# A two-block transformer step on one core: the experts' conditional branch passed before the last product, the tail split by column halves, and low parts, sines and row numbers in other places

## The reference

```python
def first_block(x, ...):
    for i in range(2):
        h = gated_deltanet(x, ...) if i == 0 else swa_sink_attention(x, ...)
        x = layer_norm(ALPHA * x + h, ln_g[i, 0], ln_b[i, 0])
        f = swiglu(x, ...) if i == 0 else moe_swiglu(x, ...)
        x = layer_norm(ALPHA * x + f, ln_g[i, 1], ln_b[i, 1])
    return x

def moe_swiglu(x, w_router, w_gate, w_up, w_down):
    top_val, top_idx = lax.top_k(xf @ w_router, 2)
    gates = ...                       # softmax of the two, one row per token
    for e in range(8):
        h = silu(xf @ w_gate[e]) * (xf @ w_up[e])
        out = out + gates[:, e:e + 1] * (h @ w_down[e])

def second_block(x, positions, ...):
    cos_a, sin_a = rope_tables(positions, 128)
    cos_i, sin_i = rope_tables(positions, 64)
    for l in range(2):
        h = rmsnorm(x, norm_g[l])
        q, k, v, ga, iq, ik, iw, xr, gr, ma, mb = split(h @ w_in[l])
        ...
        x = x + merged @ w_o[l]
    return rmsnorm(x, final_g)
```

## Time and profile before

| | us |
|---|---|
| median of 3 runs (lowest, highest) | 2206.4 (2204.94, 2208.66) |
| the profiled execution | 2202.83 |
| its span, first to last instruction | 2201.0 |
| PE busy | 2128.4 |
| VectorE busy | 1742.1 |
| ScalarE busy | 1483.7 |
| GpSimd busy | 378.1 |
| stage of the experts (560 to 1460): PE busy in 900 | 894.64 |
| 1460 to 1490: PE busy in 30 | 19.20 |

### The profile page before, as it was taken

How to read it: one execution, slowest core, us unless ns; L and a number is a source line. 1 busy time by engine, 2 the same in 40 slices (tenths; PEclk the granted TensorE clock), 3 DMA queues, 4 the chain that set the end, 5 groups by cost and what they waited for, 6 DMA issues and landing times.

```text
span 2201.0 us, 34517 instructions
## 1 busy us (share of the span) xinstructions
PE 2128.4 (97%) x13871; PEld 1888.9 (86%) x13871; DVE 1742.1 (79%) x2200; ACT 1483.7 (67%) x1982; POOL 378.1 (17%) x338
## 2 busy tenths in 40 slices
PE   8999999889999999999999999989998999999998
PEld 7988999877877888888888888869898998899898
DVE  5756555888999999999999999975698665689675
ACT  5644444556787888888888888864687844477864
POOL 0511000001002000000000000000667500458710
PEclk9999999998999999999999999989999999999999
DMA  8225855429999999999999999966555475555552
GB/s 278 97 76 122 264 192 179 157 71 349 356 336 387 395 388 390 370 394 378 376 366 394 372 390 375 386 218 202 177 172 177 129 228 184 184 159 175 158 165 98
DMA packets 326878, 564.69 MB, mean 257 GB/s; under 512 B 19872, under 2 KB 160952, under 8 KB 326712
## 3 DMA queue, kind: packets, MB, share of 16 engines
q1 hardware_dynamic: 314560, 527.60, 67.9%
q0 software_dynamic: 11760, 34.76, 5.7%
q10 hardware_dynamic: 392, 0.05, 0.0%
HBM read 548.32 MB, written 14.02 MB: 255 GB/s over the span
## 4 chain that ended last, share of the span: by engine, by line
PE 78%; DVE 10%; issue 6%; ACT 4%; POOL 1%; DMA 1%; SPq 0%; DVEq 0%; ACTq 0%; POOLq 0%
PE bank L901 24%; PE bank L903 23%; PE bank L902 23%; DVE parts L2626 3%; PE bank L907 2%; PE bank L1056 1%; ACT parts L1947 1%; PE bank L1874 1%; DVE work L3429 1%; POOL scr_f L811 1%; DVE work L3432 0%; PE bank L1834 0%; ACT work L2557 0%; DVE work L3430 0%; PE bank L1855 0%
## 5 line engine op out<-in xcount | busy, mean ns | idle before, releaser
L2626 DVE TENSOR_TENSOR parts<-raw,parts 128x1024 fp32r<-128x1024 f32 (+2 forms) x711 | 856.2, 1222 | 320.6 <-ACT parts L1947 297.3
L1947 ACT CAST parts<-raw 128x1024 fp32r<-128x1024 f32 (+2 forms) x711 | 730.5, 1036 | 404.2 <-PE bank L903 389.2
L901 PE MATMUL bank<-cols,parts 128*128 128x256 f32 x1680 | 488.9, 291 | 11.3 <-DVE work L3542 4.9
L902 PE MATMUL bank<-cols,parts 128*128 128x256 f32 x1680 | 477.8, 284 | 0.0
L903 PE MATMUL bank<-cols,parts 128*128 128x256 f32 x1680 | 477.6, 284 | 0.0
L2626 DVE TENSOR_TENSOR fast<-raw,fast 128x1024 fp32r<-128x1024 f32 x302 | 361.8, 1218 | 29.7 <-ACT fast L1947 12.9
L1947 ACT CAST fast<-raw 128x1024 fp32r<-128x1024 f32 x302 | 315.5, 1052 | 85.7 <-PE bank L903 77.3
L901 PEld LDWEIGHTS bank<-cols,parts 128*128 128x128 f32 x1680 | 323.5, 193 | 18.6 <-issue 9.9
L902 PEld LDWEIGHTS bank<-cols,parts 128*128 128x128 f32 x1680 | 323.9, 193 | 2.8 <-issue 1.9
L903 PEld LDWEIGHTS bank<-cols,parts 128*128 128x128 f32 x1680 | 323.7, 193 | 0.0
L901 PE MATMUL bank<-parts,cols 128*128 128x512 f32 x740 | 292.2, 395 | 8.0 <-DVE cols L3088 3.5
(11 more groups left out here) (433 smaller groups left out, 3385.4 us busy)
## 6 DMA issues: line engine op xcount, KB each, us to landing
raw<-in_moe_w_gate_dram SPq DMA_DIRECT2D x112, 1024.0 KB, 8.5
raw<-in_moe_w_up_dram SPq DMA_DIRECT2D x112, 1024.0 KB, 8.4
raw<-in_moe_w_down_dram SPq DMA_DIRECT2D x112, 1024.0 KB, 8.9
raw<-in_w_in_dram SPq DMA_DIRECT2D x76, 1024.0 KB, 5.3
raw<-in_a_w_in_dram SPq DMA_DIRECT2D x12, 1024.0 KB, 11.5
raw<-in_ffn_w_gate_dram SPq DMA_DIRECT2D x11, 1024.0 KB, 5.3
raw<-in_ffn_w_up_dram SPq DMA_DIRECT2D x11, 1024.0 KB, 5.4
raw<-in_ffn_w_down_dram SPq DMA_DIRECT2D x11, 1024.0 KB, 5.0
```

The source lines that it names most:

```text
L901: pe.matmul(o, l[0], r[0], start=start, stop=False)
L902: pe.matmul(o, l[0], r[1], start=False, stop=False)
L1947: a.copy(dst[0], src).then_inc(*up(o + "hi", x))
L2626: v.tensor_tensor(dst[1], src, dst[0].bitcast(F32), ALU.subtract).then_inc(*up(o + "lo", x))
```

## The change

1. **Branch.** In `experts` the last step's down product (`down(NS - 1)`) and, on VectorE, `scatter_last` are no longer in the loop but in a function `last`, which is called in the `If` arm and in a new `Else` arm, on ScalarE and VectorE. The sum of (1, 1) is a function of its own. `Signals.rewind` sets the counters back so that both arms count alike. PE's queue keeps its `If` where it was.
2. **Row numbers.** `ids` stands ahead of the last four pieces' low parts and of `product`, and waits for ScalarE's pt in place of PE's p_picked.
3. **Sines.** More `yield`s: ScalarE's sines come one step behind VectorE's angles, the second angles one step later than before.
4. **The norm behind the experts.** Both means first; the second half's LayerNorm product between the first half's gain and diagonal; the second half's gain on GpSimd (event h_rows_p); low parts and column parts alternate; PE calls `h_cols(0, 1)` inside `rm_first`, behind the third piece.
5. **First mixer.** The low parts of the pieces behind `T_qv[3]` and `T_qv[4]` (`POOL_LO`, two pieces) are GpSimd's, ahead of `level(0)`; who reads them waits for pool_lo.
6. **Tail.** The last `out_proj` does the last four pieces of t=1 by column halves (event quarter behind the first); sum, gain and squares of t=1 follow by halves (`f_deviation`).

```diff
@@ Signals
+    def rewind(self, before):
+        for family, n in before.items():
+            if not family.startswith("o_") and "_o_" not in family:
+                self.count[family] = n
@@ pieces
+    POOL_LO = W.after[T_qv[3]] + W.after[T_qv[4]]
+    def lo_name(x):
+        return "pool_lo" if x in POOL_LO else "lo"
@@ sync_program, load
-                sp.wait_ge(*at(o + "lo", W_.chunks[c - RAW]["pieces"][-1]))
+                for x in W_.chunks[c - RAW]["pieces"][-2:]:
+                    sp.wait_ge(*at(lo_name(x) if o == MAIN else o + "lo", x))
@@ pool_program
         gp.memset(N1.TT[HIGH, :, 0:64], 0.0).then_inc(*up("tt_zero"))
+        gp.wait_ge(*at("tt_zero"))
+        for y in POOL_LO:
+            src, dst = piece_view(W, y)
+            gp.wait_ge(*at("hi", y))
+            gp.tensor_tensor(dst[1], src, dst[0].bitcast(F32), ALU.subtract).then_inc(*up("pool_lo", y))
         gp.wait_ge(*at("gdn_const"))
-        gp.wait_ge(*at("tt_zero"))
         level(0)
...
+        gp.wait_ge(*at("h_gain", 0))
+        gp.wait_ge(*at("rows", 3, 1))
+        gp.tensor_tensor(HN.G[0][:, 1, :], X[:, 1, :], HN.g[0], ALU.mult).then_inc(*up("h_rows_p", 0, 1))
@@ tensor_program, out_proj
             k_.then_inc(*up("half", mine[7]))
+            if by_half:
+                for h, event in ((0, "quarter"), (1, "used")):
+                    for k in range(4, 8):
+                        k_ = step(k, 1, (h,))
+                    k_.then_inc(*up(event, mine[7]))
+                return
@@ tensor_program, second block
             if l == 0:
                 h_cols(0, 0)
-                h_cols(0, 1)
...
-            rm_first(..., ("v", l, 0), (lambda: h_cols(1, 1)) if l else None)
+            rm_first(..., ("v", l, 0), lambda l=l: h_cols(l, 1))
@@ scalar_program, experts
-            for n in range(NS + 3):
+            for n in range(NS + 1):
...
-                if 2 <= n <= NS + 1:
+                if n > 1:
                     down(n - 2)
-            return flag
+            return flag, lambda: down(NS - 1)
@@ scalar_program, setup_steps
+            yield
             yield
             for i in range(2):
                 ...
                 a.activation(co, rr, ACT.Sin).then_inc(*up("cos", i))
                 yield
+                yield
...
+        before = dict(S.count)
         with a.If(flag > 0):
+            last()
             ...
+        S.rewind(before)
+        with a.Else():
+            last()
         root_table(3)
@@ scalar_program, h_norm
+            h_deviation(l, 0)
             if l == 0:
+                his(1, 4)
+                h_hi(0, 0)
+                h_deviation(0, 1)
+                h_hi(0, 1)
+                his(4, 5)
@@ scalar_program, the end
+        def f_deviation():
+            q = LT[:, 8:16]
+            a.wait_ge(*at("resid", 1, 1, 0))
+            a.activation(HN.junk[:, 0:512], X[:, 1, 0:512], ACT.Square, accum_out=q[:, 0:1]).then_inc(*up("h_ss", 2, 1, 0))
+            a.wait_ge(*at("h_ss", 2, 1, 0))
+            a.activation(q[:, 1:2], q[:, 0:1], ACT.Identity, bias=eps["h"], scale=1.0 / D).then_inc(*up("h_ss", 2, 1, 1))
+            a.wait_ge(*at("resid", 1, 1, 1))
+            a.activation(HN.junk[:, 512:1024], X[:, 1, 512:1024], ACT.Square, accum_out=q[:, 6:7]).then_inc(*up("h_ss", 2, 1))
+            a.wait_ge(*at("h_ss", 2, 1))
+            a.activation(q[:, 7:8], q[:, 6:7], ACT.Sqrt, bias=q[:, 1:2], scale=1.0 / D).then_inc(*up("h_sd", 2, 1))
@@ vector_program, experts
             def ids(e):
-                v.wait_ge(*at("p_picked", e))
+                v.wait_ge(*at("pt", e))
...
+                if side and n == 0:
+                    ids(0)
+                if side and ahead and g == 3:
+                    ids(e + 1)
                 if n < NS:
                     for x in gu[n][4:8]:
                         after(x, W_, o)
                     product(n)
-                if side and n == 0:
-                    ids(0)
-                if side and ahead and g == 3:
-                    ids(e + 1)
...
+            def last():
+                down(NS - 1)
+                scatter_last(NE - 1)
+            return flag, last
@@ vector_program, behind the experts
+        S.rewind(before)
+        with v.Else():
+            last()
+            add_last(MAIN, NE - 1, 1, 1)
...
+        ln_mean(0)
+        ln_mean(1)
         ln_gains(0)
-        ln_gains(1)
         ln_rows(0)
         h_gains(0, 0)
+        ln_gains(1)
         h_diag(0, 0)
+        h_lows(0, 0, 1)
         ln_rows(1)
-        h_gains(0, 1)
...
@@ vector_program, the end
+                if l == t == 1:
+                    for h, event in enumerate(("quarter", "used")):
+                        cs = slice(512 * h, 512 * h + 512)
+                        v.wait_ge(*at(event, t_["o"][7]))
+                        v.tensor_tensor(X[:, t, cs], X[:, t, cs], bank[6 + h][:, :], ALU.add).then_inc(*up("resid", l, t, h))
+                        v.wait_ge(*at("resid", l, t, h))
+                        v.tensor_tensor(HN.G[2][:, t, cs], X[:, t, cs], HN.g[2][:, cs], ALU.mult).then_inc(*up("h_rows", 2, t) if h else up("dve"))
```

137 lines of the change are left out of this document (74 added, 63 removed).

## The result

The changed kernel takes 2196.22 us, the median of 6 runs (2195.75 to 2198.88), beside 2206.78 for the kernel before, measured with it (6 runs, 2204.94 to 2208.66). The ratio is 0.9955, with an interval from 0.9945 to 0.9965. The forecast was 2197.3, with a range from 2194.0 to 2203.5. A second measurement gave 2197.69 (6 runs); over all 12 runs the median is 2196.6.

A forecast was written before the change was run, and what follows sets the result against it. TensorE, busy 97%, was taken as the bound, so gains come from its gaps and the ends: mixer 0.7, experts 5.36, norm 2.0 with branch, tail 1.1, sum 9.1 us, from 2206.4 to 2197.3; range 2194.0 to 2203.5.

The forecast's parts named there:

- it gives 2193.7 for a profile: Whole kernel: the 9.1 us gain taken off the 2201.0 us span of the profiled execution of before.
- Branch, 1.84: Behind the experts: early compare hides the jump's 1.89 us under VectorE's wait for y; gain 1.84, from 0 to 1.89.
- Rival A: Behind the experts: the 1.89 gap returns at the Else arm's end or was never the jump; 2199.2 us; 20%.
- The norm's order, 0.1: Norm behind the experts: reorder by itself gains 0.1 us; the stage gives 2.0, branch included.
- piece 1 at 1481.1: Second block's norm: time when piece 1 is ready for v0, needed by PE at 1482.4 on the earlier timeline.
- it is not held up: Second block's norm: PE gets every piece of v0's first token block before it needs it.
- Row numbers, 2.56: Expert stage: earlier row numbers close PE's gaps of 0.86 and 1.70; gain 2.56 us, from 1.7 to 2.56.
- sines, 2.80: Expert stage: sines a step behind angles close PE's gap at 627.82; gain 2.80 us, from 0.
- rival B: Expert stage: weight stream or VectorE's backlog takes the 5.36 us back; 2202.6 us; 14%.
- GpSimd's low parts, 0.7: First mixer: two low parts on GpSimd let the third block's mask begin earlier; gain 0.7 us, from 0 to 1.5.
- The tail, 1.1: Kernel's end: column halves leave 1.92 us behind PE's last matmul instead of 3.02; gain 1.1, from 0.8 to 1.2.
- Rival C: Norm: TensorE stays at 1.2 GHz until v0 is done, losing 12.7 us; slower than before, 2210.0 us; 4%.

The follow-up runs named there:

- branch_alone: Kernel before with only the branch part: last product step and sums in both arms, compare ahead of them; 2203.86 us, ratio to before 0.9992.
- second_if: Changed kernel with a second compare and nearly empty If body on VectorE between last sum and mean; 2194.13 us in its one run.
- u_rows: Changed kernel with the row numbers behind the low parts and the product again, sines a step behind as changed; 2199.73 us.
- u_sines: Changed kernel with the sines right beside the angles again, row numbers early as changed; 2201.38 us.
- u_lo: Changed kernel with all low parts of the first mixer on VectorE again, none on GpSimd; 2196.42 us.

## Why the prediction was right, and where it was not

**The sum.** 9.1 us were forecast on the median, and 10.6 came in the first measurement, 9.2 by the 12 runs of the changed kernel beside 2205.8. The sign, the size and the likeliest case were right. That the total came so near is partly luck: the norm and the tail were taken too large (1.1 to 1.7 came in place of 2.0, and 0.1 to 1.0 in place of 1.1), the expert stage too small (7.0 by the medians in place of 5.36). The forecast took 9.1 off the span of one trace as well; there 6.4 came, because that trace of before had only one dip that cost time and the rare order in the mixer, while the usual execution is 3 us longer and its second trace 5.3. The step "it gives 2193.7 for a profile" (2196.42 came) failed for this reason, and the median did not.

**Branch, 1.84.** Right, and the best founded term: branch_alone's gap of 7.66 is the 7.7 forecast to the tenth. Rival A with its 20% (the gap comes back at the end of the `Else` arm) fell: 0.61 us from sum to mean. The sentence from the Trainium skill (Advanced Engine Details and Errata, Control Flow Timing), 51 and 108 ns for a branch and a compare, is not contradicted: an estimate from its two figures is 0.16 us together, and that can pass unseen in second_if while the last sum runs for 0.68. It does not hold for the far jump, 1.89 and 2.38 us here, which the sum rightly took from the row.

**The norm's order, 0.1, and the v0 feed.** The gap in front of the norm fell by 2.18, and 0.2 of it is the order's. But the term as a whole had the wrong sign: behind the gap the order lost 1.0, so it cost 0.8. The step that failed is "piece 1 at 1481.1" and, with it, "it is not held up". Piece 0, the second LayerNorm row and the low columns came at the forecast distances; the low part of piece 1 came 1.6 us later (1476.20, where 1481.1 less the 6.5 us by which PE began earlier is 1474.6). PE was held up for the low part of piece 1, for 1.05 us in a trace whose clock was back by then and under a slower clock in the next one, since I gave GpSimd's product its slowest duration (2.96 in the earlier trace rows) and no effect on VectorE. Those 2.96 were the lock already: 1.06 of them, beside the 1.90 that the product takes by itself, were the wait for the low part at 77.27 that starts 0.01 us ahead. The row had the answer, in two instructions of two engines side by side whose times don't add up to what either takes elsewhere. The stage gave 1.7 in place of 2.0 by the ledger, and 1.1 beside the second trace of before (9.50 + 17.02 us became 7.46 + 18.0).

**Row numbers, 2.56, and sines, 2.80.** The gaps went as forecast, and nothing came in their place: PE is busy for all of 560 to 1460, so rival B fell. Mis-sized are both terms: 1.05 + 1.89 and 3.10 in the ledger, where the restart is counted, and 3.1 and 4.8 in the medians of u_rows and u_sines, where some executions also lose clock behind the gap. The step that failed is to take a gap for its idle time. The third gap also varies by itself, from 1.70 to 2.36 in the three traces of the old stage.

**GpSimd's low parts, 0.7.** Right at the place (1.49 became 0.78, the start 0.70 earlier) and in the comparison with u_lo (0.70). That these two parts hold VectorE as well (VectorE's L2837 at 51.85 took 1.94 in place of 0.30, under GpSimd's 51.24 to 53.64) was not seen; it cost nothing at the end of the chain, since ScalarE's decays come last there.

**The tail, 1.1.** 1.0 on the engines, and in half of the traces 0.1 at the end of the span. The forecast ended its sum at the last scaling, and the stores behind it were taken as fixed; they are not.

**Rival C.** Fell: the second h_cols took 1.95 us for 16 matmuls at full clock. The clock mattered all the same, at other places and in small pieces. Its "some 35 matmuls at half clock" don't follow from 9 us: at 0.229 each these are 39, or 31 beside the 1.8 of the second h_cols; nothing hangs on it.

## What to carry to other kernels

Before an instruction goes to GpSimd, look at what VectorE does in the same microseconds: if both read SBUF alone, one of them may wait for the other, and a pair that starts 0.01 us apart may take either order from one execution to the next. A far jump at the end of a stage can be passed early, under a wait that is there anyway, by writing the stage's last step into both arms. Count a short gap of TensorE for more than its idle time: the restart, and in some executions the clock behind it. And judge a reorder by when the stage ends, not by the gap ahead of it: here a shorter gap stood in front of a longer stage.

## What the runs showed of the hardware

- Behind gaps of TensorE of 0.9 to 2.8 us the granted clock fell to its lower level (1.2 GHz) for some 3 to 5 us in some executions and stayed at 2.4 GHz in others of the same program. A dip costs 1.5 us here (5 dips, 7.7 us), or nothing where a wait on another engine follows (0.58 us in place of 1.29), and 1 to 7 of them stand in a trace. They are most of the spread between traces of one kernel.
- In the pairs looked at, VectorE and GpSimd exclude each other for a whole instruction where both have only operands in SBUF (1.21 becomes 2.97, 0.30 becomes 1.94, 1.21 becomes 2.80; GpSimd's 1.90 becomes 2.96), and do not where VectorE reads PSUM (2.42 for six taps of the convolution, with and without GpSimd's 1.89 beside it).
- A jump over some 380 rows costs 1.89 to 2.38 us on VectorE, a short one nothing that shows.
- The last stores of 0.25 MB land in 2.3 or in 3.2 us, five times each with column halves, and in 2.3 in all four traces with whole rows.
